# A hybrid block and a gated block on one core: the second layer's first four tiles on unnormalised input, with the norm applied to their results

## The reference, cut to what matters

```python
def layernorm(x, g, b):
    mu = mean(x); var = mean((x - mu) ** 2)
    return (x - mu) * rsqrt(var + LN_EPS) * g + b

def hybrid_layer(x, ...):                 # D_MODEL 2048, 512 tokens
    proj = x @ w_in                       # q_lat, kv_lat, k_rope, gates, pool and conv inputs
    ...                                   # attention, pooling, convolution, gates
    out = mix @ w_out + b_out
    return layernorm(DEEPNORM_ALPHA * x + out, ln_g, ln_b)

h = layernorm(x, emb_ln_g, emb_ln_b)
for l in range(2):
    h = hybrid_layer(h, ...)
# then one second block: rms_norm with modulation silu(c) @ w_ada + b_ada,
# spatial gating, forgetting attention, output projection, final rms_norm
```

## Time and profile before

| | us |
|---|---|
| median of three runs (2501.84 to 2504.44) | 2502.83 |
| the profiled execution, its own time | 2505.22 |
| its span | 2503.5 |
| TensorE busy | 2414.2 (96%) |
| VectorE busy | 1259.9 (50%) |
| ScalarE busy | 890.3 (36%) |
| GpSimd busy | 396.5 (16%) |

### The profile page before, as it was taken

How to read it: one execution, slowest core, us unless ns; L and a number is a source line. 1 busy time by engine, 2 the same in 40 slices (tenths; PEclk the granted TensorE clock), 3 DMA queues, 4 the chain that set the end, 5 groups by cost and what they waited for, 6 DMA issues and landing times.

```text
span 2503.5 us, 31553 instructions
## 1 busy us (share of the span) xinstructions
PE 2414.2 (96%) x11534; PEld 1977.2 (79%) x11534; DVE 1259.9 (50%) x1794; ACT 890.3 (36%) x1344; POOL 396.5 (16%) x391
## 2 busy tenths in 40 slices
PE   4999999999999999999999999899999999999997
PEld 2888888788888788888788886688878888887886
DVE  8665543366446565444366546635245444444333
ACT  4522222365223522222365223322234444444221
POOL 6400000033003300000042003003002122222000
PEclk8999999999999999999999999999999999999999
DMA  4455554212221455553212222322222222223332
GB/s 141 149 182 169 183 177 133 77 60 67 93 92 67 156 185 170 175 184 126 83 52 68 92 92 101 126 93 93 100 93 68 76 79 80 75 75 100 127 101 75
DMA packets 78280, 277.69 MB, mean 111 GB/s; under 512 B 8832, under 2 KB 9088, under 8 KB 77824
## 3 DMA queue, kind: packets, MB, share of 16 engines
q1 hardware_dynamic: 61344, 213.29, 25.8%
q0 software_dynamic: 16864, 63.45, 7.6%
HBM read 268.31 MB, written 8.39 MB: 111 GB/s over the span
## 4 chain that ended last, share of the span: by engine, by line
PE 80%; issue 9%; DVE 5%; POOL 3%; ACT 2%; DMA 0%; DVEq 0%; ACTq 0%; SPq 0%; POOLq 0%
PE bank L322 25%; PE bank L324 25%; PE bank L323 25%; POOL sum L407 1%; DVE w_lo L317 1%; PE bank L1898 1%; DVE x_lo L1037 1%; POOL probs L394 1%; PE bank L1828 1%; ACT w_hi L294 0%; PE bank L1962 0%; PE bank L1679 0%; PE bank L1680 0%; DVE x_res L1598 0%; PE bank L1963 0%
## 5 line engine op out<-in xcount | busy, mean ns | idle before, releaser
L324 PE MATMUL bank<-x_hi,w_hi 128*128 128x512 f32 x2880 | 1125.6, 391 | 0.0
L323 PE MATMUL bank<-x_hi,w_lo 128*128 128x512 f32 x2880 | 1124.1, 390 | 0.0
L322 PE MATMUL bank<-x_lo,w_hi 128*128 128x512 f32 x2368 | 946.7, 400 | 30.7 <-DVE x_lo L1037 17.2
L317 DVE TENSOR_TENSOR w_lo<-w_raw,w_hi 128x1024 fp32r<-128x1024 f32 (+1 forms) x384 | 483.6, 1262 | 792.7 <-ACT w_hi L294 791.1
L294 ACT ACTIVATE w_hi<-w_raw 128x1024 fp32r<-128x1024 f32 x390 | 407.5, 1048 | 950.6 <-PE bank L324 926.9
L324 PEld LDWEIGHTS bank<-x_hi,w_hi 128*128 128x128 f32 x2880 | 542.0, 188 | 115.3
L323 PEld LDWEIGHTS bank<-x_hi,w_lo 128*128 128x128 f32 x2880 | 543.4, 189 | 107.8 <-issue 2.4
L322 PEld LDWEIGHTS bank<-x_lo,w_hi 128*128 128x128 f32 x2368 | 447.7, 189 | 124.6 <-issue 30.9
L322 PE MATMUL bank<-mix_lo,w_hi 128*128 128x512 f32 x640 | 252.8, 395 | 1.3 <-issue 1.0
L394 POOL TENSOR_SCALAR probs<-probs,stats 128x128 f32<-128x128 f32 (+3 forms) x128 | 138.6, 1089 | 672.7 <-DVE stats L1329 672.6
L322 PEld LDWEIGHTS bank<-mix_lo,w_hi 128*128 128x128 f32 x640 | 120.7, 189 | 27.2 <-issue 1.7
(11 more groups left out here) (304 smaller groups left out, 2268.9 us busy)
## 6 DMA issues: line engine op xcount, KB each, us to landing
w_raw<-stream SPq DMA_DIRECT2D x390, 512.0 KB, 3.5
ada_w<-wada POOLq DMA_DIRECT2D x96, 512.0 KB, 4.6
x_res<-xT SPq DMA_DIRECT2D x16, 256.0 KB, 5.5
x_res_spill<-x_res POOLq DMA_DIRECT2D x8, 512.0 KB, 7.5
x_res<-x_res_spill POOLq DMA_DIRECT2D x8, 512.0 KB, 7.5
outT<-x_res SPq DMA_DIRECT2D x16, 256.0 KB, 2.3
cond_b<-cond POOLq DMA_DIRECT2D x2, 1024.0 KB, 5.2
row_params<-rows POOLq DMA_DIRECT2D x1, 1536.0 KB, 7.5
```

Of the source, the lines that this page charges most:

```text
L317: nc.vector.tensor_tensor(out=WL[:, slot, :cols[n]], in0=RAW[:, slot, :cols[n]], in1=WH[:, slot, :cols[n]].bitcast(F32), op=ALU.subtract). ...
L322: nc.tensor.matmul(out, wh, xl, start=first, stop=False)
L323: nc.tensor.matmul(out, wl, xh, start=False, stop=False)
L324: return nc.tensor.matmul(out, wh, xh, start=False, stop=last)
```

## The change

The second hybrid layer (l = 1, `RAW_LAYER`) starts with four tiles instead of three, on input that is centred by a shift and multiplied by `ln_g`, but not normalised. VectorE and ScalarE form its two parts during the output tiles of layer 0 (`raw_hi`, `raw_lo`); `raw_tiles` on TensorE follows the last output tile with no gap in its list, and the token sums and spreads stand inside it. VectorE then takes the four banks, subtracts mean times weight sum and multiplies by the reciprocal deviation (`raw_tile`), and ScalarE adds the other weight sum. The normalisation of the 16 feature tiles stays, and runs beside these tiles. The weight sums of the four tiles, with g and with b, are made by VectorE in layer 0 from transposed weights (`weight_sums`, 16 instructions of 128x1024, from 8 loads of 512 KB and 2 of 1 MB), on the last 8 of the 28 steps; the 48 sums of `ada` of layer 0 are dealt over the first 20. In both layers the centring becomes part of `x_res` itself: GpSimd subtracts the shift from 14 tiles beforehand, VectorE from two, and the separate subtraction at L971 goes. The roles of the two activation buffers are swapped in layer 1, the ring of weight slots runs on across layers instead of starting anew, and one split moves from behind the norm's multiply to before it in layer 1's end.

```diff
+RAW_LAYER, RAW_TILES = 1, 4
+RAW_BANKS = (0, 3, 4, 6)
...
+                if l + 1 == RAW_LAYER:
+                    pool.wait_ge(S["ada_done"], ADA_LAYER * (l + 1))
+                    for n in range(2 * RAW_TILES):
+                        if n:
+                            pool.wait_ge(S["wt_done"], 2 * n)
+                        if n % RAW_TILES == 0:
+                            pool.dma_start(CONDB[:, :], lnrows[n // RAW_TILES].broadcast_to([P, 2 * UNIT]))\
+                                .then_inc(S["wt_rows"], 16)
+                        pool.dma_start(ADAB[:, 0, :], wt[n]).then_inc(S["wt_in"], 16)
...
+                pool.wait_ge(S["sh_b"], l + 2)
+                for k in range(2, KT):
+                    nc.gpsimd.tensor_tensor(out=Y[:, k, :], in0=Y[:, k, :], in1=SB[:, :], op=ALU.subtract)\
+                        .then_inc(S["ysub"], 1)
...
+                for i in range(raw):
+                    if i == 2:
+                        split(l, 5)
...
+                    act.wait_ge(S["lat_raw"], 2 * (i + 1))
...
+                    nc.scalar.activation((T0, Y1)[i % 2][:, :], LAT[:, i, :], ACT.Square, scale=-1.0,
+                                         bias=VEC[:, 2 * i + 1:2 * i + 2]).then_inc(S["in_ev"], 1)
+                    nc.scalar.activation(LAT[:, i, :], LAT[:, i, :], ACT.Identity, scale=-1.0,
+                                         bias=VEC[:, 2 * i + 1:2 * i + 2]).then_inc(S["lat_hi"], 1)
+                    if i < 2:
+                        split(l, 4, (i,))
...
-                    for n in range(ADA_LAYER * (s - 5) // (T_GATE - 3), ADA_LAYER * (s - 4) // (T_GATE - 3)):
+                    late = l == RAW_LAYER
+                    steps = T_GATE - 3 - (0 if late else 2 * RAW_TILES)
+                    first = ADA_LAYER * (s - 5 - (late and s == 6)) // steps
+                    for n in range(first, min(ADA_LAYER * (s - 4 - (late and s == 5)) // steps, ADA_LAYER)):
                         ada(l, n)
+                    if not late and s - 5 >= steps:
+                        weight_sums(s - 5 - steps)
...
-                TT(out=CT[:, :], in0=feature(Y, k), in1=SB[:, :], op=ALU.subtract).then_inc(S["ct"], 1)
-                dve.wait_ge(S["ct"], KT * n + k + 1)
-                TT(out=A1[:, :], in0=A1[:, :], in1=CT[:, :], op=ALU.add).then_inc(S["sum1"], 1)
+                TT(out=A1[:, :], in0=A1[:, :], in1=Y[:, k, :], op=ALU.add).then_inc(S["sum1"], 1)
...
+            def raw_lo(n, k):
+                dve.wait_ge(S["raw_hi"], k + 1)
+                dve.wait_ge(w_used, n * LAYER_UNITS - (k < 8))
+                STT(out=LO[n][:, k, :], in0=Y[:, k, :], scalar=col(n - 1, C_LG + k), in1=HI[n][:, k, :].bitcast(F32),
+                    op0=ALU.mult, op1=ALU.subtract).then_inc(S["raw_lo"], 1)
...
+            def raw_tile(l, t):
+                dve.wait_ge(w_used, first_done(l, t))
+                dve.wait_ge(S["n_x"], norm_uses(l, KT - 1))
+                STT(out=LAT[:, t, :], in0=SB[:, :], scalar=VEC[:, 2 * t:2 * t + 1], in1=PS[RAW_BANKS[t]][:, :],
+                    op0=ALU.mult, op1=ALU.subtract).then_inc(S["lat_raw"], 1)
+                dve.wait_ge(S["lat_raw"], 2 * t + 1)
+                TT(out=LAT[:, t, :], in0=LAT[:, t, :], in1=PS[7][:, :], op=ALU.mult).then_inc(S["lat_raw"], 1)
...
+                if raw:
+                    raw_sums()
+                    raw_tile(l, 0)
+                    split(l, 4, (0,))
+                    raw_tile(l, 1)
+                    split(l, 4, (1,))
+                    raw_tile(l, 2)
+                    raw_tile(l, 3)
+                    split(l, 5)
...
+            def raw_tiles(l):
+                tiles = range(RAW_TILES)
+                order = [(k, t) for k in range(2) for t in tiles[:-1]] + [(k, tiles[-1]) for k in range(2)]
+                order += [(k, t) for k in range(2, 6) for t in tiles]
+                order += [(k, t) for t in tiles for k in (6, 7)] + [(k, t) for t in tiles for k in range(8, 11)]
+                order += [(k, t) for k in range(11, KT) for t in tiles]
...
+                    if t == RAW_TILES - 1:
+                        if k == 1:
+                            column_totals(l)
+                        elif k == 2:
+                            spreads(l)
...
-                norm_sums(l + 1)
-                fill(26)
+                if l + 1 != RAW_LAYER:
+                    norm_sums(l + 1)
+                    fill(26)
```

More of the change, by code:

```diff
@@ L56 @@
 MIX_ORDER = [0, 1, 2, 3, 4, 5, 12, 13, 8, 9, 10, 11, 6, 14, 15, 7]
+OUT_ORDER = (MIX_ORDER, list(range(16)))
 LAT_TILES = ((8, 2), (9, 3), (10, 4), (11, 5), (12, 0), (13, 1))
@@ L111, in poff, with build @@
     return P * i * (i + 1) // 2
-def build(nc, layers, extra, stream, wada, wsT, wpool, rows, cond, positions, invf, xT, outT):
+def build(nc, layers, extra, stream, wada, wsT, wpool, rows, cond, positions, invf, xT, wt, lnrows, outT):
     from contextlib import ExitStack
@@ L1122, in layer @@
                 sums = 0
+                raw = RAW_TILES if l == RAW_LAYER else 0
+                if raw:
[7 more added lines that the diff above has]
+                    split(l, 5)
                 for i in range(6):
                     m = T_KV + i
-                    if ahead(m):
+                    if ahead(m) and i >= raw:
                         split(l, ahead(m))
-                    if i == 0:
+                    if i == 0 and not raw:
                         split(l, 3)
@@ L1133, in layer @@
                         sums += 1
-                    if i == 1:
+                    if i == 1 and not raw:
                         split(l, 4)
@@ L1276, in out_tile @@
                 def out_tile(m, i=0):
-                    if m < KT - 1:
-                        split(l, T_OUT + m + 2, (0,), i)
-                    dve.wait_ge(w_used, step_done(l, T_OUT + m, i))
+                    split(l, T_OUT + m + 2, (0,))
+                    if m == KT - 1 and l + 1 == RAW_LAYER:
+                        for k in range(8):
+                            raw_lo(l + 1, k)
+                    dve.wait_ge(w_used, step_done(l, T_OUT + m))
                     if m == 0:
                         dve.wait_ge(S["res"], KT * (l + 1))
-                    y = feature(Y, m + 2 * i)
-                    TT(out=y, in0=y, in1=PS[m % 2][:, :], op=ALU.add).then_inc(S["out_ev"], 1)
+                    if m >= 2:
+                        dve.wait_ge(S["ysub"], (KT - 2) * l + m - 1)
+                    TT(out=Y[:, m, :], in0=Y[:, m, :], in1=PS[m % 2][:, :], op=ALU.add).then_inc(S["out_ev"], 1)
                     if m == 1:
+                        dve.wait_ge(S["out_ev"], KT * l + 2)
                         dve.wait_ge(S["zero"], 2 * (l + 1))
@@ L1707, in layer @@
             def layer(l):
                 def in_tile(m, mid={}, i=0):
-                    if m not in (T_KR, 3):
+                    raw = RAW_TILES if l == RAW_LAYER else 0
+                    if raw and m == T_KR:
+                        pe.wait_ge(S["lat_raw"], 2 * raw)
+                    elif raw and m == raw + 1:
+                        pe.wait_ge(S["in_ev"], taken(l, 0))
+                    elif m not in (T_KR, raw or 3):
                         pe.wait_ge(S["in_ev"], taken(l, m - 2) + 2 * i)
-                    tile(l, m, {T_KR: 7, 3: FIRST_BANKS[3]}.get(m, m % 2), mid=mid, i=i)
+                    banks = {T_KR: 7, raw: 1, raw + 1: 0} if raw else {T_KR: 7, 3: FIRST_BANKS[3]}
@@ L1714, in pool_mm @@
+                    tile(l, m, banks.get(m, m % 2), (S["x_lo_s"], KT * l) if m == raw and raw else None,
+                         mid=mid, i=i)
                 def pool_mm(j):
@@ L2057, with first_order @@
 IN_COLS_2 = {"u": 0, "v": 1024, "g_a": 2048, "q": 3072, "k": 4096, "v_b": 5120, "g_b": 6144, "f": 7168}
-def first_order(tiles):
-    first, rest = tiles[:3], tiles[3:]
+def first_order(tiles, count=3):
+    first, rest = tiles[:count], tiles[count:]
     return [t[0] for t in first] + [t[1] for t in first] + [u for t in rest for u in t]
```

264 lines of the change are left out of this document (168 added, 96 removed).

## The result

| | before | after |
|---|---|---|
| median, us | 2502.35 (2501.84 to 2504.44, 4 runs) | 2527.18 (2524.79 to 2528.18, 4 runs) |
| profiled execution, its span | 2505.22, 2503.5 | 2524.79, 2523.2 |
| TensorE busy | 2414.2 | 2408.2 (95%) |
| VectorE busy | 1259.9 | 1295.6 (51%) |
| GpSimd busy | 396.5 | 454.3 (18%) |

The ratio is 1.0096, 95% interval 1.0079 to 1.0114: the change makes the kernel slower, by 24.8 us on the medians. The forecast was +27.7, to 2530.5.

The account below looks back on a forecast made before the run. TensorE was taken as the bound, time being won or lost only where it waits. 14.4 + 14.8 - 1.5 = 27.7 us added to 2502.8 gave 2530.5, with a range of 2513 to 2539.

Parts of the forecast that it names:

- clock behind them, to layer 1's attention: Behind TensorE's late arrival at the q sums of layer 1: 1.7 us lost to a lower granted clock.
- Part 1: Layer 0: bunched modulation sums make TensorE wait 3.65, 2.5 and 3.2 us; with 5.1 for the clock, 14.4 us lost.
- steps of three: Layer 0 steps with three modulation sums on two buffers; the third waits for a reload, holding VectorE 5.2 us.
- Part 2: Boundary between layers 0 and 1: late raw tiles, a stall before tile 4 and late q sums; 14.8 us lost with clock.
- The tail without the stream: Between the raw tiles' end and tile 4: activations, corrections and splits take 7.3 us, so tile 4 could start at 845.0.
- if it is again let in behind the fifteenth: Before tile 4: `w_lo` is held within GpSimd's 16 residual instructions until ahead of the sixteenth; tile 4 starts 8.7 us later.
- The sign that I had set: Near 860 of the new span: a TensorE wait of 7 us or more (by the forecast 16) on `w_lo`.
- rival A: At the boundary: GpSimd's stream holds VectorE for one instruction at most; 8.0 us less, 2522.5. Chance 0.27.
- B: Layer 0 chains are not late, boundary as in Part 2; 13.3 us more than before, 2516. Chance 0.10.
- C: Modulation loads land before they are asked and GpSimd lets `w_lo` in at once; 9.1 us gained, 2494. Chance 0.08.
- D: The two sides cancel within 5 us: C's loads, but clock losses and late low parts stay; 2500.5. Chance 0.07.
- Part 3: Second boundary: moved subtraction, earlier mean to GpSimd and moved split together gain 1.5 us, between 0 and 3.

Follow-up runs that it names:

- the repeat: The changed kernel, not edited, run again beside the kernel before: 2528.47 us against 2504.5, ratio 1.0092.

## Why the prediction was right, and where it was wrong

Positions in the trace give the terms one by one. The places are transposes of the probabilities late in each layer's attention (these rows, before and after), the q sums, and the first product of the second block. In the repeat they stand at 624.65, 904.88, 1381.01 and 1602.37.

```profile
606.24 0.44 PE L1828 MATMUL bank<-ident,probs 128*128 128x128 f32 x2 [0.95 <-POOL probs L394]
...
1353.65 0.44 PE L1828 MATMUL bank<-ident,probs 128*128 128x128 f32 x2 [0.94 <-POOL probs L394]
```

```profile
621.47 0.44 PE L1982 MATMUL bank<-ident,probs 128*128 128x128 f32 x2 [0.94 <-POOL probs L415]
...
1377.30 0.44 PE L1982 MATMUL bank<-ident,probs 128*128 128x128 f32 x2 [0.94 <-POOL probs L415]
...
1598.61 0.77 PE L343 MATMUL bank<-x_lo,w_hi 128*128 128x512 f32 x1 [7.25 <-DVE x_lo L1456]
```

| term, us | predicted | profiled execution | its repeat |
|---|---|---|---|
| layer 0 | +14.4 | +15.2 | +18.4 |
| boundary to the q sums | +13.1 | +5.2 | +5.6 |
| clock behind them, to layer 1's attention | +1.7 | +3.2 | +3.3 |
| second boundary | -1.5 | -2.8 | -2.7 |
| behind it, not touched | 0 | -1.2 | -1.2 |
| sum | +27.7 | +19.7 | +23.4 |

**Part 1, layer 0: right in mechanism, place and waits, with one term left out.** Predicted waits 3.65, 2.5 and 3.2; measured 3.50, 2.28 and 3.62, and in the repeat 3.09, 2.26 and 4.68. Taking away the steps of three took them all away. The other steps of three and the weight sums cost nothing, as said. The clock behind the waits was put at 1.7 each, 5.1 in all. By the positions it cost 3.4, 0.2 and 1.5 in the profiled execution, 5.2 in all, and 1.8, 1.8 and 2.9 in the repeat: the sum is about right, and how it falls on the three places changes from run to run. What the forecast put at nothing is the loss ahead of the q sums, 1.9 and 2.1 us, which goes with the earlier place of the kv sums and the slow clock behind them (read from positions; no run puts the old place back). And 1.3 and 0.3 us less were lost in layer 0's attention, where TensorE idles 3.0 us in every kernel and the clock behind it differed between the executions; the change does not touch that place. So the 15.2 is 1.9 + 9.4 + 5.2 - 1.3.

**Part 2, the boundary: right in its chain, wrong in one term.** The raw tiles' end was forecast 53.4 us after 784.3; it came 53.0 after the same point shifted by layer 0's 15.2. The tail without the stream was to be 7.3, and was 7.8. From tile 4's start to the q sums the forecast had 13.0 + 27.2 = 40.2 us; it was 901.28 - 860.81 = 40.5, ended by the sum that the forecast named. The step that failed is "if it is again let in behind the fifteenth", worth 8.7 us: `w_lo` lost 0.5. I had taken one row for a property of the stream, when its asking came 6.5 us in; the runs show that one 1.4 us in gets in after 0.5 us. The sign that I had set, a TensorE wait of 7 us or more for tile 4, could not tell the two apart, since the chain without the hold gives 7.3 by itself; the low part of about 9 us inside the stream was the sign that could, and it did not come. The hold itself is real: it costs the kernel before 5.5 us over both layers, and it struck as forecast when the asking came 4.7 us in.

The Trainium skill ("SBUF — State Buffer", "Who interferes with whom") has the lock held for one whole instruction. If VectorE gets in behind the GpSimd instruction that it meets, that bounds the loss at 0.69, and the 0.5 in the trace agrees. But it would bound every hold so, and the low parts that were asked at 4.7 us lost 5.8 (four in 10.56, where two undisturbed take 2.36). So this bound does not hold for a train of instructions, of which the section says nothing.

**So rival A's mechanism happened, inside a sum that had other errors.** A's own sum, 27.7 - 8.0 = 19.7, is just what the spans of the two profiled executions differ by, though there too its terms miss by 0.8, 0.1, 1.5, -1.3 and -1.2 and cancel. In time A gave 2522.5; the median was 2527.2, nearer to the forecast's 2530.5. The profiled execution after is 2.4 below its median, and the repeat shows where such microseconds lie: layer 0 and the clock behind the q sums cost 4.0 and 1.6 more there than costed, against 0.8 and 1.5. And the forecast took 2.4 off for the profiled execution before, which in the end lay 2.9 above its median. That the forecast's time came closer than A's is luck: one term of 8 us too large, against others that were too small.

**Rivals B, C and D** are out. B needed layer 0's chains in time, and C and D loads that land before they are asked: the 40 us before `ada` say no. C's idea was sound in another sense: with VectorE's order mended the deferral gains 10.7 us, where C had 9.1.

**Part 3** was -2.8 instead of -1.5, inside its bounds of 0 to 3. No run parts its three terms, and the cause of the -1.2 behind it, where nothing was changed, is open.

## What to carry to other kernels

When work is taken from the critical engine, look at what the change does to the order of the helper engine: here the whole loss came back when no three sums stood in a row on two buffers near a deadline, and the gain showed when the splits and the residual stream were out of each other's way too. A pair of buffers that is refilled on use served two uses for nothing and made the third wait for the rest of its reload (4.16 us at step 7), so count uses between two deadlines, not uses per layer. Look also at how far a consumer moved: a wait grew from 1.31 to 2.60 us when its place came six products sooner, and a slow clock followed. A hold seen once has a phase; before it is put into a sum, ask whether the new program meets it at the same phase.

## What was not expected of the hardware

- An unbroken train of 16 GpSimd instructions (0.69 us each) kept out VectorE's two-input SBUF operation for up to 6 us, in every case where its first asking came 4.6 us or more after the train's start; at 3.1 us or less it got in at an edge, and so did the later ones in the same train, which stretched by 2.0 to 4.4 us. Corrections with an operand in PSUM, 0.73 to 0.75 us each, were never held.
- Cutting such a train in two, with nothing else changed, made the kernel before 0.23% faster (0.14 to 0.32%).
- The length of a wait alone does not tell what the clock does. Behind 2.28 us (201.82) it stayed at 1.00 for 6 us; in the repeat, behind 2.26 us at the same place, it was 0.72, then 0.50, then 0.92 in three windows of 2 us. Behind 8.32 and 6.77 us it was at 0.50 for 5 to 6 us, behind 3.50 us at 0.57 and 0.50 for 6 us, but behind 3.09 us at the same place in the repeat at 0.66 and 0.77. In the kernel before, 1.31 us in layer 0 left it at 1.00, and 1.20 us in the earlier trace rows was followed, 2 us later, by 0.53 for 3.6 us.
